# Groups of stick-breaking heads moved in among the last projections of a layer

## The chip, the cores and the metric

One NeuronCore of a Trainium2 chip runs the whole program. The metric is device time in microseconds (us), the median of several executions of the same program; lower is better. Five engines work from queues of their own, each strictly in its written order: TensorE (PE) multiplies, ScalarE (ACT) applies functions and copies, VectorE (DVE) does elementwise work, GpSimd (POOL) and SyncE (SP) mostly start transfers. They meet only at semaphores.

## The reference

256 tokens of width 1024 pass through two transformer layers and a third block, all in fp32. The second layer's mixer (`mixer_cd`) is the place of the change:

```python
def mixer_cd(h, w_in, w_out, rel_table):
    proj = h @ w_in                      # columns: qc, kc, vc, qd, kd, vd
    ...
    o_c = moba_attention(...)            # 8 heads; at 256 tokens: causal softmax with a bias
    o_d = stick_breaking_attention(...)  # 8 heads
    return jnp.concatenate([o_c, o_d], axis=-1) @ w_out

def stick_breaking_attention(q, k, v):
        z = jnp.einsum('bqhd,bkhd->bhqk', qb, k).astype(jnp.float32) * scale
        strict = kpos[None, :] < tq[:, None]
        log_1m = jnp.where(strict, jax.nn.log_sigmoid(-z), 0.0)
        after = lax.cumsum(log_1m, axis=3, reverse=True) - log_1m
        w = jnp.where(strict, jnp.exp(jax.nn.log_sigmoid(z) + after), 0.0)
        o = jnp.einsum('bhqk,bkhd->bqhd', w.astype(dt), v)
```

## The kernel before

**Weights.** SP loads chunks of 1 MB (`raw`, five buffers, L2032). Each chunk has two halves; ACT rounds a half to `HI` (`high`, L940 is the helper of every activation), DVE takes the rest, `LO = raw - HI` (`low`, L1352), and PE multiplies with both. Six half-chunks fit in `HI`/`LO` at once. `Walk` is the planner that all engines run alike: `use(key, half)` prepares the half-chunk four places ahead of the one named, if its slot is free, and along the way DVE multiplies chunks of the modulation matrices (`gemv`, L1342). `walk.spare(n)` takes up to n modulation halves, if these are the next in the plan. Where this layer's attention calls it the next chunk is a weight (`cdo` 2), so there it does nothing.

**The layer, in order.** `linear_fm` makes projections `cd` 0 to 5 (queries and keys, into `FMT`), `values_only` makes `cd` 6 and 7 (values of the stick-breaking heads), `keys_values` makes `cd` 8 (keys and values of the softmax heads). ACT copies each out of PSUM when it is complete. Then comes the attention, six rounds on each engine.

- The softmax heads are six units, taken in pairs: `scores` (PE), `biased` (DVE: bias and row maximum), `exps` (ACT), `scaled` (DVE), `transposes` (PE), `moved` (ACT, out of PSUM), `values` (PE).
- The stick-breaking heads are four groups g of two heads: `stick_scores` (PE makes z; DVE adds the mask, L1740; ACT takes abs, exp and ln, three passes of 768 columns), `stick_sums` (DVE forms the logarithms, L1746; PE sums them over the keys; DVE adds, L1749; ACT takes exp), `stick_values` (PE). `stage` deals two of these steps to each round: groups 0 and 1 go through all three steps, then groups 2 and 3.
- PSUM has four working banks (`take`/`give`), handed out in turn. PE waits in `take` until the reader of a bank's last content is done.
- Two sets of buffers (`stick_flat`) hold z, a and the logarithms l of a group, so group g shares with g - 2. Groups 0 and 1 use the queries and keys of `cd` 2 and 4, groups 2 and 3 those of `cd` 3 and 5.

**After it.** When the last `values` is done, ACT copies the four accumulator banks to `HH` (`out_parts` 0 to 3), DVE makes `HLo` (L1434), and `out_half("cdo", (0, ..., 5), 0)` multiplies with the output matrix. It needs parts 0 and 1 before its first matmul. ACT then makes the SiLU of a condition row and goes on with the weights.

## Time and profile before

| | |
|---|---|
| median of 3 executions | 1266.91 us (1266.78 to 1272.68) |
| the profiled execution's own time | 1268.52 us |
| its span, first to last instruction | 1266.7 us |
| mean granted TensorE clock | 0.965 |
| PE busy | 1159.9 us, 92% |
| PE weight loads busy | 1049.2 us, 83% |
| DVE busy | 933.0 us, 74% |
| ACT busy | 589.4 us, 47% |
| POOL busy | 74.4 us, 6% |

Times in the trace are us from the span's start. The projections of this layer run from 406.4 to 462 us, the attention from 462 to 503.9, the output matrix from there to 528.
### The profile page before, as it was taken

To read this page: it belongs to the slowest core of one execution; us is meant where nothing else is said; L and a number is where in the kernel's file an instruction comes from. 1 tells how busy PE (TensorE), PEld (TensorE's weight loads), DVE (VectorE), ACT (ScalarE), POOL (GpSimd) and SP (SyncE) were. 2 spreads that over 40 slices of the span, in tenths; PEclk is the share of its full clock that TensorE was granted. 3 is DMA by queue.
4 is the path that set the end of the run, shared out by engine and by line. 5 is a ranking of instruction groups with operands and counts; after the bars stand their busy time and mean duration, and the time that the engine had idled before them with its cause. 6 is when DMAs were issued, how large, how long until landed. Compare 5 with 4: busy or idle time off the path is not lost.

```text
span 1266.7 us, 19978 instructions
## 1 busy us (share of the span) xinstructions
PE 1159.9 (92%) x8358; PEld 1049.2 (83%) x8358; DVE 933.0 (74%) x1630; ACT 589.4 (47%) x968; POOL 74.4 (6%) x106
## 2 busy tenths in 40 slices
PE   2798798999998977899999989999989988999996
PEld 1687468999897975699999979999979967999996
DVE  5967868888786955598888688887765957765445
ACT  1534655434355455554445464454452365444443
POOL 0000000000000000079000000000000000000000
PEclk8799899999999989999999999999999998999998
DMA  9982335788882960357889637779732452665730
GB/s 375 364 358 74 152 128 196 299 319 286 310 331 100 374 225 1 136 203 277 315 202 368 245 139 296 293 273 292 279 140 101 105 177 85 254 233 200 194 133 34
DMA packets 40810, 280.83 MB, mean 222 GB/s; under 512 B 4736, under 2 KB 5264, under 8 KB 7952
## 3 DMA queue, kind: packets, MB, share of 16 engines
q1 hardware_dynamic: 37296, 269.27, 58.5%
q0 software_dynamic: 2416, 7.92, 2.2%
q10 hardware_dynamic: 1008, 2.37, 0.5%
q8 instruction: 65, 1.06, 0.3%
q14 instruction: 25, 0.20, 0.1%
HBM read 277.91 MB, written 1.10 MB: 220 GB/s over the span
## 4 chain that ended last, share of the span: by engine, by line
PE 69%; DVE 19%; ACT 6%; DMA 5%; issue 1%; SPq 0%; DVEq 0%; ACTq 0%
PE PS L408 68%; DVE LO L1352 5%; DMA raw<-WS 4%; DVE raw L1342 4%; ACT HI L940 2%; DMA SC<-scratch 1%; DVE TMP L1417 1%; DVE SC L1556 1%; DVE TMP L1452 1%; DVE HLo L1412 1%; ACT HH L940 1%; ACT SQ L940 1%; ACT SC L940 1%; DVE SC L1541 1%; DVE RS L1556 1%
## 5 line engine op out<-in xcount | busy, mean ns | idle before, releaser
L408 PE MATMUL PS<-HH,HI 128*128 128x256 f32 x1748 | 502.0, 287 | 25.6 <-ACT HH L940 22.3
L408 PE MATMUL PS<-HLo,HI 128*128 128x256 f32 x1748 | 503.3, 288 | 0.9 <-DVE HLo L1412 0.3
L408 PE MATMUL PS<-HH,LO 128*128 128x256 f32 x1748 | 499.3, 286 | 0.0
L1352 DVE TENSOR_TENSOR LO<-raw,HI 128x1024 fp32r<-128x1024 f32 x340 | 403.8, 1226 | 116.1 <-ACT HI L940 115.9
L940 ACT ACTIVATE HI<-raw 128x1024 fp32r<-128x1024 f32 x340 | 339.8, 1048 | 93.8 <-PE PS L408 64.8
L408 PEld LDWEIGHTS PS<-HH,HI 128*128 128x128 f32 x1748 | 340.0, 195 | 34.9 <-DVE LO L1352 18.9
L408 PEld LDWEIGHTS PS<-HLo,HI 128*128 128x128 f32 x1748 | 339.3, 194 | 4.2 <-DVE HLo L1412 2.9
L408 PEld LDWEIGHTS PS<-HH,LO 128*128 128x128 f32 x1748 | 339.8, 194 | 3.4 <-issue 0.5
L1342 DVE CUSTOM_DVE_ANT_0 raw<-raw,CB,SM 128x1024 f32<-128x1024 f32 x168 | 210.5, 1285 | 24.5 <-DMA raw<-WS 24.5
L408 PE MATMUL PS<-HI,HDH 128*128 128x512 f32 x352 | 140.4, 399 | 0.0
L408 PE MATMUL PS<-HI,HDL 128*128 128x512 f32 x352 | 139.6, 397 | 0.0
L408 PE MATMUL PS<-LO,HDH 128*128 128x512 f32 x352 | 138.9, 395 | 0.0
L940 ACT ACTIVATE HDH<-FB 128x256 fp32r<-128x256 f32 x88 | 36.8, 418 | 210.1 <-DVE FB L1513 210.0
L940 ACT ACTIVATE FB<-PS 128x256 f32<-128x256 f32 (+1 forms) x94 | 37.8, 403 | 129.4 <-PE PS L408 129.3
L408 PEld LDWEIGHTS PS<-HI,HDL 128*128 128x128 f32 x352 | 66.4, 189 | 15.9
L940 ACT ACTIVATE SC<-PS 128x512 f32<-128x512 f32 (+3 forms) x65 | 36.2, 572 | 90.0 <-PE PS L408 68.5
L408 PEld LDWEIGHTS PS<-LO,HDH 128*128 128x128 f32 x352 | 66.5, 189 | 12.8
L408 PEld LDWEIGHTS PS<-HI,HDH 128*128 128x128 f32 x352 | 66.5, 189 | 12.6 <-DVE LO L1352 0.2
L1513 DVE TENSOR_TENSOR FB<-FB,PS 128x256 f32<-128x256 f32 x88 | 36.7, 416 | 52.1 <-ACT FB L940 52.0
L408 PE MATMUL PS<-HI,HH 128*128 128x512 f32 (+2 forms) x176 | 62.3, 354 | 10.2 <-DVE HLo L1434 5.8
L1516 DVE TENSOR_TENSOR HDL<-FB,HDH 128x256 fp32r<-128x256 f32 x88 | 37.7, 428 | 45.9 <-ACT HDH L940 45.9
L408 PE MATMUL PS<-LO,HH 128*128 128x512 f32 (+2 forms) x176 | 61.4, 349 | 0.0
(230 smaller groups left out, 1023.1 us busy)
## 6 DMA issues: line engine op xcount, KB each, us to landing
raw<-WS SPq DMA_DIRECT2D x255, 1024.0 KB, 5.5
SC<-scratch POOLq DMA_DIRECT2D x2, 1024.0 KB, 13.4
FB<-gates_out POOLq DMA_DIRECT2D x3, 512.0 KB, 5.1
SQ<-gates_out POOLq DMA_DIRECT2D x3, 512.0 KB, 9.4
X<-xT ACTq DMA_DIRECT2D x1, 1024.0 KB, 6.9
SC<-ssm POOLq DMA_DIRECT2D x2, 512.0 KB, 5.0
out<-TMP SPq DMA_DIRECT2D x2, 512.0 KB, 2.6
CB<-vecs SPq DMA_DIRECT2D x1, 512.0 KB, 6.5
```

The costliest lines, as they stand in the source:

```text
L408: return e.matmul(o, l, r, start=start, stop=stop, skip_group_check=True)
L940: return e.activation(o, a, f, **k)
L1342: e.tensor_tensor_reduce(x, x, CB[:, :], 1.0, S("mb")[:, c:c + 1], O.mult, O.add, MV[:, c:c + 1]) \
L1352: e.tensor_tensor(LO[:, s % HL, :], raw_half(j, h), HI[:, s % HL, :].bitcast(fp32), O.subtract).then_inc(*D.up(("lo", s)))
L1412: e.scalar_tensor_tensor(HLo[:, k, :], TMP[:, k, :], MV[:, sh + k:sh + k + 1], HH[:, k, :].bitcast(fp32), O.add, O.subtract).then_inc(*D.u ...
L1417: e.scalar_tensor_tensor(TMP[:, k, :], turned(k), AV[:, k:k + 1], RS[:, 3, :], O.mult, O.mult) \
L1452: e.tensor_tensor(gy[qt][:, c], PS[:, b, :], grow(tag)[:, c], O.mult).then_inc(*D.up(("gy", tag, b)))
L1513: e.tensor_tensor(HF[:, j % 2, :], SIL[:, j % 2, :], bank((key, 0))[:, 256:512], O.mult) \
L1516: e.tensor_tensor(HDL[:, j % 3, :], HF[:, j % 2, :], HDH[:, j % 3, :].bitcast(fp32), O.subtract) \
L1541: e.tensor_scalar(s3[:, n, :], s3[:, n, :], gg[:, n:n + 1], None, O.mult) \
L1556: e.tensor_tensor_reduce(s3[:, n, :], bank(("s", tag, i))[:, n * kw:(n + 1) * kw], BI[:, bh + h0 + n, bo:bo + kw], 1.0, sk[:, n:n + 1] if ...
```

## The change

On all three compute engines the six rounds and their `stage` list are replaced by a written order:

- `stick_scores(0)` stands right after the projections 0 to 5, `stick_scores(1)` between the halves of `cd` 6, `stick_sums(0)` between those of `cd` 7, `stick_scores(2)` after `cd` 7, `stick_sums(1)` and `stick_values(0)` between the halves of `cd` 8, `stick_sums(2)` after it. `keys_values` and `values_only` get an argument `between` for this on PE; ACT and DVE have their parts and their `use` calls written out in the matching order.
- The logarithms are written over a (`af`), so that three sets of buffers fit. Group g now shares with g - 3.
- The remaining units (`stick_scores(3)`, the values of 1, 2 and 3, the sums of 3, and all of the softmax heads) are in an order written by hand. `out_parts` 2 and 3, which depend only on the stick-breaking heads, are copied before the last softmax values.
- PE waits in `stick_scores` for the projections it reads, and in `stick_values(0)` and `(1)` for the copied values.

```diff
@@ -358,8 +358,8 @@
         AB = dense(0, 10, 0, 0, 0, gate=1, last=False) + dense(0, 11, 128, 0, 0, gate=2) \
             + dense(4, 12, 256, 8, 2, sink=True)
         CD = dense(0, 12, 0, 0, 0)
-        stick_flat = [(SC[:, 11904:12672], SC[:, 6656:7424], SC[:, 7424:8192]),
-                      (sqf[:, 0:768], sqf[:, 768:1536], flat(TMP[:, 0:3, :]))]
+        stick_flat = [(SC[:, 11904:12672], SC[:, 6656:7424]), (sqf[:, 0:768], sqf[:, 768:1536]),
+                      (SC[:, 7424:8192], flat(TMP[:, 0:3, :]))]
         stick_cube = [[x.rearrange("p (h n) -> p h n", h=2) for x in f] for f in stick_flat]
 
         Wv = [WVT[:, i, :] for i in range(22)]
@@ -477,19 +477,23 @@
                         i = mm(o(qt), l[0], x[1], False, stop and k == ks[-1])
                 i.then_inc(*P.up(("lin", key, half), used(key, half)))
 
-            def keys_values(key):
+            def keys_values(key, between=()):
                 ps = take((key, 0))
                 wt = [x.rearrange("p (k n) -> p k n", k=8) for x in weight(key, 0)]
                 for k in range(8):
                     i = mm3(ps[:, 0:256], [x[:, k, :] for x in wt], H2[k], k, k == 0, k == 7, key[0])
                 i.then_inc(*P.up(used(key, 0)))
+                for f, g in between:
+                    f(g)
                 wt = [x.rearrange("p (k n) -> p k n", k=8) for x in weight(key, 1)]
                 linear_tm(lambda qt: ps[:, 256 + qt * 128:384 + qt * 128], key, 1, range(8), wt, False, True)
                 banks.give((key, 0))
 
-            def values_only(key):
+            def values_only(key, between=()):
                 ps = take((key, 0))
                 for half in range(2):
+                    for f, g in between if half else ():
+                        f(g)
@@ -777,12 +781,10 @@
             modulate("cd", 56, (8, 4, 4))
             for i in range(6):
                 linear_fm(("cd", i), H2, "cd", 8, 2)
-            for i in range(2):
-                values_only(("cd", 6 + i))
-            keys_values(("cd", 8))
 
             def stick_scores(g):
                 ps = [take(("ss", g, i)) for i in range(2)]
+                w.wait_ge(*A.at(("proj", "cd", 4 + g // 2)))
                 for kt in range(2):
                     for i in range(2):
                         hs = slice(i * 64, i * 64 + 64)
@@ -794,7 +796,7 @@
                     banks.give(("ss", g, i))
 
             def stick_sums(g):
-                l3 = stick_cube[g % 2][2]
+                l3 = stick_cube[g % 3][1]
                 for i in range(2):
                     ps = take(("sc", g, i))
                     w.wait_ge(*D.at(("sf", g)))
@@ -804,8 +806,10 @@
                     banks.give(("sc", g, i))
 
             def stick_values(g):
-                a3 = stick_cube[g % 2][1]
+                a3 = stick_cube[g % 3][1]
                 w.wait_ge(*A.at(("sa", g)))
+                if g < 2:
+                    w.wait_ge(*A.at(("v", g)))
                 for kt in range(2):
                     for i in range(2):
                         c = 128 + (2 * g + i) * 64
@@ -813,21 +817,31 @@
                                a3[:, i, kt * 256:256 + kt * 128], kt == 1)
                 x.then_inc(*P.up(("sv", g)))
 
-            stage = [(f, g) for g0 in (0, 2) for f in (stick_scores, stick_sums, stick_values) for g in (g0, g0 + 1)]
-
-            def two_stages(i):
-                for f, g in stage[2 * i:2 * i + 2]:
-                    f(g)
-
-            for i in range(6):
-                if i < 3:
-                    scores("cd", CD, i)
-                if 1 < i < 5:
-                    transposes("cd", i - 2)
-                walk.spare(2)
-                two_stages(i)
-                if i > 2:
-                    values("cd", CD, i - 3)
+            stick_scores(0)
+            values_only(("cd", 6), [(stick_scores, 1)])
+            values_only(("cd", 7), [(stick_sums, 0)])
+            stick_scores(2)
+            keys_values(("cd", 8), [(stick_sums, 1), (stick_values, 0)])
+            stick_sums(2)
+            scores("cd", CD, 0)
+            walk.spare(2)
+            stick_scores(3)
+            stick_values(1)
+            scores("cd", CD, 1)
+            walk.spare(2)
+            stick_values(2)
+            transposes("cd", 0)
+            stick_sums(3)
+            scores("cd", CD, 2)
+            walk.spare(2)
+            transposes("cd", 1)
+            values("cd", CD, 0)
+            walk.spare(2)
+            stick_values(3)
+            values("cd", CD, 1)
+            transposes("cd", 2)
+            walk.spare(4)
+            values("cd", CD, 2)
             out_half("cdo", (0, 1, 2, 3, 4, 5), 0)
             out_half("cdo", (0, 1), 1)
             out_half("cdo", (6, 7), 0)
...
@@ -1122,8 +1132,12 @@
                                 .then_inc(*DUPED.up("in", by=16))
                 if n in (2, 4):
                     flip(n // 2 - 1)
+            use(("ab", 6), 0)
+            use(("ab", 6), 1)
             keys_values(("ab", 6), 0, "kv6")
-            values_only(("ab", 7), 128, ("fm", "ab"))
+            use(("ab", 7), 0)
+            use(("ab", 7), 1)
+            values(("ab", 7), 128, ("fm", "ab"))
             w.wait_ge(*P.at("gates"))
             fn(ge, bank("gates")[0:24, 0:256], F.Exp, scale=-1.0).then_inc(*A.up(("free", "gates")))
 
@@ -1202,12 +1216,9 @@
                 use(("cd", i), 0)
                 use(("cd", i), 1)
                 evacuate(("cd", i), flat(FMT[:, 2 * i:2 * i + 2, :]), ("proj", "cd", i), 0.125 if i < 2 else 1.0)
-            for i in range(2):
-                values_only(("cd", 6 + i), 128 + 256 * i, ("v", i))
-            keys_values(("cd", 8), 0, ("fm", "cd"))
 
             def stick_scores(g):
-                zf, af, lf = stick_flat[g % 2]
+                zf, af = stick_flat[g % 3]
                 w.wait_ge(*D.at(("sz0", g, 1)))
                 fn(af, zf, F.Abs).then_inc(*A.up())
                 w.wait_ge(*A.now())
@@ -1215,32 +1226,51 @@
                 w.wait_ge(*A.now())
                 fn(af, af, F.Ln, bias=1.0).then_inc(*A.up(("sl", g)))
 
-            def stick_sums(g):
-                zf, af, lf = stick_flat[g % 2]
+            def stick_weights(g):
+                zf, af = stick_flat[g % 3]
                 w.wait_ge(*D.at(("sz", g, 1)))
                 fn(af, zf, F.Exp).then_inc(*A.up(("sa", g)))
 
-            def stick_values(g):
-                pass
-
-            stage = [(f, g) for g0 in (0, 2) for f in (stick_scores, stick_sums, stick_values) for g in (g0, g0 + 1)]
-
-            def two_stages(i):
-                for f, g in stage[2 * i:2 * i + 2]:
-                    f(g)
-
-            for n in range(6):
-                for i in (2 * n - 4, 2 * n - 3):
-                    if 1 < n < 5:
-                        moved("cd", i)
-                for i in (2 * n, 2 * n + 1):
-                    if n < 3:
-                        exps("cd", i, *CD[i])
-                high(walk.spare(2))
-                two_stages(n)
+            use(("cd", 6), 0)
+            use(("cd", 6), 1)
+            stick_scores(0)
+            values(("cd", 6), 128, ("v", 0))
+            stick_scores(1)
+            use(("cd", 7), 0)
+            use(("cd", 7), 1)
+            values(("cd", 7), 384, ("v", 1))
+            stick_weights(0)
+            use(("cd", 8), 0)
+            use(("cd", 8), 1)
+            stick_scores(2)
+            stick_weights(1)
+            keys_values(("cd", 8), 0, ("fm", "cd"))
+            stick_weights(2)
+            exps("cd", 0, *CD[0])
+            exps("cd", 1, *CD[1])
+            high(walk.spare(2))
+            stick_scores(3)
+            exps("cd", 2, *CD[2])
+            exps("cd", 3, *CD[3])
+            high(walk.spare(2))
+            moved("cd", 0)
+            moved("cd", 1)
+            stick_weights(3)
+            high(walk.spare(2))
+            moved("cd", 2)
+            moved("cd", 3)
+            exps("cd", 4, *CD[4])
+            exps("cd", 5, *CD[5])
+            high(walk.spare(2))
+            w.wait_ge(*P.at(("sv", 3)))
+            out_parts("cdo", 2)
+            out_parts("cdo", 3)
+            high(walk.spare(4))
+            moved("cd", 4)
+            moved("cd", 5)
             w.wait_ge(*P.at(("v", "cd", 5)))
-            for i in range(4):
-                out_parts("cdo", i)
+            out_parts("cdo", 0)
+            out_parts("cdo", 1)
             w.wait_ge(*C2IN.at("cond"))
             fn(CB[:, :], CB[:, :], F.Silu).then_inc(*A.up("cact"))
             e.preload_act_table_set(LNEXP)
@@ -1727,49 +1757,74 @@
             ffn("f0", rates(), 4, "cd", (40, 1.0, S("nw")[:, 24:32]))
             add_normed("cd", "f0", 56, S("nw")[:, 32:40], False)
             modulate("cd", 48)
-            for i in range(9):
+            for i in range(6):
                 use(("cd", i), 0)
                 use(("cd", i), 1)
 
             def stick_scores(g):
-                zm = stick_cube[g % 2][0]
+                zm = stick_cube[g % 3][0]
                 for i in range(2):
                     w.wait_ge(*P.at(("ss", g, i)))
-                    if g > 1:
-                        w.wait_ge(*P.at(("sv", g - 2)))
+                    if g > 2:
+                        w.wait_ge(*P.at(("sv", g - 3)))
                     e.scalar_tensor_tensor(zm[:, i, :], bank(("ss", g, i))[:, 0:384], 0.125, C("smask"), O.mult,
                                            O.add).then_inc(*D.up(("free", ("ss", g, i)), ("sz0", g, i)))
 
+            def stick_logs(g):
+                zf, af = stick_flat[g % 3]
+                w.wait_ge(*A.at(("sl", g)))
+                e.scalar_tensor_tensor(af, zf, 0.0, af, O.max, O.add).then_inc(*D.up(("sf", g)))
+
             def stick_sums(g):
-                (zf, af, lf), zm = stick_flat[g % 2], stick_cube[g % 2][0]
-                w.wait_ge(*A.at(("sl", g)))
-                e.scalar_tensor_tensor(lf, zf, 0.0, af, O.max, O.add).then_inc(*D.up(("sf", g)))
+                zm = stick_cube[g % 3][0]
                 for i in range(2):
                     w.wait_ge(*P.at(("sc", g, i)))
                     e.tensor_tensor(zm[:, i, :], zm[:, i, :], bank(("sc", g, i))[:, 0:384], O.add) \
                         .then_inc(*D.up(("free", ("sc", g, i)), ("sz", g, i)))
 
-            def stick_values(g):
-                pass
-
-            stage = [(f, g) for g0 in (0, 2) for f in (stick_scores, stick_sums, stick_values) for g in (g0, g0 + 1)]
-
-            def two_stages(i):
-                for f, g in stage[2 * i:2 * i + 2]:
-                    f(g)
-
+            def unit(f, i):
+                f("cd", i, *CD[i])
+
+            use(("cd", 6), 0)
+            stick_scores(0)
+            use(("cd", 6), 1)
+            stick_scores(1)
+            stick_logs(0)
+            use(("cd", 7), 0)
+            stick_sums(0)
+            stick_logs(1)
+            use(("cd", 7), 1)
+            stick_scores(2)
+            use(("cd", 8), 0)
+            stick_sums(1)
+            stick_logs(2)
+            use(("cd", 8), 1)
             gate("f1", 64, 1.0, S("nw")[:, 40:48])
-            for n in range(6):
-                for i in (2 * n, 2 * n + 1):
-                    if n < 3:
-                        biased("cd", i, *CD[i])
-                for i in (2 * n - 2, 2 * n - 1):
-                    if 0 < n < 4:
-                        scaled("cd", i, *CD[i])
-                low(walk.spare(2))
-                two_stages(n)
-            for i in range(4):
-                out_parts("cdo", i)
+            stick_sums(2)
+            unit(biased, 0)
+            unit(biased, 1)
+            low(walk.spare(2))
+            stick_scores(3)
+            unit(biased, 2)
+            unit(biased, 3)
+            unit(scaled, 0)
+            unit(scaled, 1)
+            low(walk.spare(2))
+            stick_logs(3)
+            unit(scaled, 2)
+            unit(scaled, 3)
+            low(walk.spare(2))
+            stick_sums(3)
+            unit(biased, 4)
+            unit(biased, 5)
+            low(walk.spare(2))
+            unit(scaled, 4)
+            unit(scaled, 5)
+            low(walk.spare(4))
+            out_parts("cdo", 2)
+            out_parts("cdo", 3)
+            out_parts("cdo", 0)
+            out_parts("cdo", 1)
             linear_out("cdo", range(8))
             add_normed("f1", "cdo", 80, S("nw")[:, 48:56], True)
             modulate("f1", 72)
```

## Rows read from the trace of the kernel before

**Rows 1.** Busy time by stretch: stretch, its us, each engine's busy us (instructions), PEclk, DMA share, GB/s
```profile
406.40:462.00 55.60, 55.58 (x448) 54.99 (x448) 44.00 (x60) 23.96 (x31) 1.46 (x2) 0.97 0.84 331
462.00:503.90 41.90, 26.16 (x192) 20.17 (x193) 24.58 (x83) 26.22 (x60) 0.54 (x1) 0.88 0.07 14
```

**Rows 2.** Waits of TensorE from 462 to 504 us: total us, times, longest
```profile
PE PS L408 <- DVE SC L1746: 7.0, 2, 5.1
```

**Rows 3.** Timeline of TensorE: start us, us, engine, line, operation, out<-in, count [idle before <-releaser]
```profile
466.59 0.92 PE L408 MATMUL PS<-SC 64*128 64x256 f32 x8 [1.95 <-DVE SC L1556]
...
479.89 0.70 PE L408 MATMUL PS<-TMP,CN 128*128 128x256 f32 x2 [1.51 <-DVE TMP L1746]
...
481.84 1.13 PE L408 MATMUL PS<-SC 64*128 64x256 f32 x8
...
482.90 1.09 PE L608 MATMUL PS<-CN,SC 128*128 128x128 f32 x8
...
483.93 0.87 PE L408 MATMUL PS<-SC 128*64 128x256 f32 x8
...
484.63 0.82 PE L408 MATMUL PS<-SQ,SC 128*64 128x256 f32 x8
...
503.92 0.47 PE L408 MATMUL PS<-HI,HH 128*128 128x512 f32 x1 [2.14 <-ACT HH L940]
```

**Rows 4.** Timeline of ScalarE, columns as before
```profile
442.31 0.60 ACT L940 ACTIVATE SC<-PS 128x512 f32<-128x512 f32 x1 [3.27 <-PE PS L408]
...
448.56 2.00 ACT L940 ACTIVATE HI<-raw 128x1024 fp32r<-128x1024 f32 x2
...
466.95 0.39 ACT L940 ACTIVATE SC<-SC 128x128 f32<-128x128 f32 x1
...
468.49 2.58 ACT L940 ACTIVATE SC<-SC 128x768 f32<-128x768 f32 x3
...
473.46 0.49 ACT L940 ACTIVATE SC<-SC 128x256 f32<-128x256 f32 x1
...
479.00 0.84 ACT L940 ACTIVATE SC<-SC 128x768 f32<-128x768 f32 x1 [3.48 <-DVE SC L1749]
...
483.60 1.08 ACT L940 ACTIVATE SC<-PS 128x512 f32<-128x512 f32 x2 [0.22 <-PE PS L608]
...
501.86 2.06 ACT L940 ACTIVATE HH<-PS 128x512 fp32r<-128x512 f32 x4 [1.86 <-PE PS L408]
```

**Rows 5.** Timeline of VectorE
```profile
463.99 0.35 DVE L1556 CUSTOM_DVE_ANT_0 SC<-PS,SC,eps 128x128 f32<-128x128 f32 x1 [6.02 <-PE PS L408]
...
466.55 1.01 DVE L1740 SCALAR_TENSOR_TENSOR SC<-PS,CN 128x384 f32<-128x384 f32 x2
...
469.71 0.48 DVE L1556 CUSTOM_DVE_ANT_0 SC<-PS,SC,eps 128x256 f32<-128x256 f32 x1 [1.17 <-PE PS L408]
...
471.72 0.17 DVE L1535 RECIPROCAL SC<-SC 128x4 f32<-128x4 f32 x1
...
473.71 0.95 DVE L1746 SCALAR_TENSOR_TENSOR SC<-SC 128x768 f32<-128x768 f32 x1
...
476.89 0.55 DVE L1749 TENSOR_TENSOR SC<-SC,PS 128x384 f32<-128x384 f32 x1 [2.23 <-PE PS L408]
...
485.21 0.62 DVE L1541 TENSOR_SCALAR SC<-SC 128x256 f32<-128x256 f32 x2
...
502.49 2.48 DVE L1434 TENSOR_TENSOR HLo<-PS,HH 128x512 fp32r<-128x512 f32 x4 [3.37 <-ACT HH L940]
```

**Rows 6.** Busy time by stretch again, columns as in rows 1: three stretches of the attention and after
```profile
474.80:478.40 3.60, 3.57 (x12) 3.02 (x12) 0.55 (x1) 0.72 (x4) 0.00 (x0) 0.55 0.00 0
...
490.00:500.00 10.00, 6.47 (x48) 5.29 (x48) 4.14 (x7) 6.81 (x10) 0.00 (x0) 1.00 0.00 0
...
505.15:508.80 3.65, 3.65 (x11) 2.82 (x9) 0.11 (x1) 3.61 (x5) 0.00 (x0) 0.53 0.02 4
```

**Rows 7.** Timeline of GpSimd: the transfer that fetches the gate row for f1
```profile
469.73 0.54 POOL L1939 DMA_DIRECT2D FB<-gates_out  x1 [10.56 <-DMA gates_out<-GV]
```

More of the change, by code:

```diff
@@ L1004, in keys_values @@
             def keys_values(key, dst, ev):
-                use(key, 0)
-                use(key, 1)
                 ps = bank((key, 0))
@@ L1011, in keys_values, with values @@
                     .then_inc(*A.up(("free", (key, 0)), ev))
-            def values_only(key, dst, ev):
-                use(key, 0)
-                use(key, 1)
+            def values(key, dst, ev):
                 w.wait_ge(*P.at(("lin", key, 1)))
```

## The prediction

> **What bounds the kernel now.** I first read the busy times by stretch and then who waits in the weak stretch. In the projections (406.4 to 462 us) PE is busy 55.58 of 55.60 us, DVE 44.0 and ACT 24.0. In the attention (462 to 503.9) PE is busy 26.2 of 41.9 us, DVE 24.6, ACT 26.2 [rows 1]. So the first stretch is bound by PE and has room on the other two; the second is bound by no engine but by a chain that passes from one to another. The waits of PE say where: 7.0 us of its 15.7 idle us are waits for the logarithms of L1746, one of them 5.1 us [rows 2]. The transfers bound neither: in the attention the DMA engines are busy 7% [rows 1], because the five buffers are full.
>
> **What moves, and its price on PE.** A change of order removes no matmul. Moved in among the projections are three times `stick_scores`, twice `stick_sums`, once `stick_values`. `stick_scores` is 8 records that take 0.92 us with the tail of the last, 0.8 to the next start. `stick_sums` runs from 479.89 to 481.84, 1.95 us at the full clock. `stick_values` runs from 483.93 to 484.63, 0.7 us [rows 3]. Sum: 3 x 0.8 + 2 x 1.95 + 0.7 = 7.0 us. As PE has no gap there, its projections end 7.0 us later, at 469.0. In return the three groups' waits for DVE and ACT should lie beside 20 us of projection work, and the attention starts with one group's weights made and two groups' nearly so.
>
> **Do the moved steps wait inside the projections?** `cd` 5 ends at about 442.3 (its copy starts at 442.31), and a projection takes some 5.8 us, a half of `cd` 6 or 7 so 2.88 (the copy in [rows 4]; 48 of the 448 records that take 55.6 us in [rows 1] for cd 5, the same for the others but cd 8). PE: scores(0) to 443.1, scores(1) at 445.9, sums(0) at 452.5, scores(2) at 457.3, sums(1) at 461.0, values(0) at 463.0, end of `cd` 8 at 469.0, sums(2) there. What each needs, with a pair of mask additions at 0.95 us (1.01 with the last one's tail) [rows 5], the three ACT passes at 2.5 and a last exp at 0.84 [rows 4], the logarithms at 0.95 and an addition at 0.55 [rows 5]:
> - ACT rounds the halves of `cd` 8 until 444.8, as it does `cdo` 0 at 448.56 now [rows 4]; DVE takes the rests at 443.9 and 446.0 with the mask of group 0 between them (446.0). ACT has a, exp and ln of group 0 at 448.6, DVE the logarithms at 449.6: 2.9 us before sums(0).
> - ACT is then held until 449.6 by the copy of `cd` 6, does group 1 until 452.8 and only then the halves of `cdo` 0 (454.8). DVE waits for them, so its additions for group 0 end at 456.1 and the logarithms of group 1 at 457.1: 3.9 us before sums(1). The bank that scores(2) takes is free at 455.6, 1.7 us early; this is the tightest one.
> - The weights of group 0 are ready at 458.9 (values(0): 463.0), the logarithms of group 2 at 464.6 (sums(2): 469.0).
>
> All have 1.7 us or more to spare, so I cost the insertions at nothing beyond PE's 7.0 us. If the cover were gone, a miss would stand one to one on PE. Between the two shapes of matmul the trace shows no exchange as such; bounds for each insertion are 0 (the steps of 479 to 485 follow without a gap, rows 3) and 0.1 us, so 0 to 0.6 us in all. I take 0.
>
> **The moved halves and queues.** On ACT and DVE the splitting of `cdo` 0 and 1 now stands behind stick work and ends at 458.3 and 465.8, some 6 to 8 us later than now. The output matrix is not touched before 492. SP's next loads wait for these rests and start as much later; the attention leaves the DMA engines idle [rows 1], so they land well ahead. The gate row for f1 is written and fetched by POOL: the fetch starts at 469.73 now, after 10.56 us of waiting for its write [rows 7]; its factor is formed 8 us later, so the fetch starts at some 478, and the row is wanted only behind the output matrix. The last modulation product ends at 452.0 by this order; its reader, the SiLU, stands behind out_parts. All hidden. The logarithms written over a are the same instruction on 768 columns: 0 (below nothing there is no reason either, since read and written sizes stay).
>
> **The attention that is left,** from the same prices. A 4-head unit costs DVE 1.28 us in `biased` (463.99 to 466.55 for two) and 1.0 in `scaled` (471.72 to 473.71 for two); a 2-head unit 1.0 (469.71 to 471.72 for two) and 0.7 (0.62 for its two multiplications, and a reciprocal) [rows 5]. `exps` costs ACT 1.55 (466.95 to 468.49 for a 4-head unit's last four passes) or 0.98 (two of 0.49), `moved` 0.5 [rows 4]. On PE a pair's scores take 1.06, its transposes 1.03 [rows 3], its values 0.8 like the 8 records of rows 3.
> - sums(2) until 471.0, scores of pair 0 until 472.0, scores(3), values(1) until 473.5. DVE adds for group 2 until 471.7, then biased 0 and 1 until 474.7. The scores of pair 1 need the bank of unit 1: 474.6 to 475.7, then values(2).
> - DVE is now the bound: mask of group 3 (475.6), biased 2 and 3 (477.8), scaled 0 and 1 (479.8), logarithms of group 3 (480.8; ACT's ln is there at 479.2). PE turns units 0 and 1 as they come and does sums(3) from 480.85 to 482.8.
> - Scores of pair 2 until 483.9, transposes of pair 1, values 0, values(3), values 1 until 487.2. DVE: biased 4 and 5 until 486.0. ACT: exps 4 and 5 until 487.6. DVE: scaled 4 and 5 at 487.4 and 488.4. PE: transposes until 488.9. ACT: out_parts 2 and 3 in between, then moved 5 until 489.75. PE: values of pair 2 from 489.8, and ACT's out_parts 0 at 490.9.
> - From there to the first output matmul it is 503.92 - 501.86 = 2.06 us, as now [rows 3, 4]: parts 0 and 1 were always the ones that PE waited for, so having 2 and 3 done early saves nothing here. The start is at 492.95.
>
> That is 503.92 - 492.95 = 11.0 us earlier at the full clock. Behind it the output matrix, f1 and the rest have the same work and waits, shifted as a whole.
>
> **The clock.** From 474.8 to 478.4 the granted clock is 0.55 and sums(0) takes 3.6 us instead of 1.95, after a PE that was idle 5.1 us [rows 2, 6]. From 490 to 500 PE is busy 65% and the clock stays at 1.00 [rows 6]. In my order PE is busy about 3.2 of the 6.9 us from 473.5 to 480.4, its longest gap 2.5 us. That lies between the two rows; nearer to the first by its share. A fall then meets sums(3), on the path, for 3.55 - 1.95 = 1.6 us (bounds 0 and, with the next scores also at half, 2.7). I take 1.6. After the last values the clock falls already now, 0.53 from 505.15 to 508.80, which costs about 1.65 us [rows 6]; PE is idle as long there as before, so I leave that in.
>
> **Sum:** -11.0 + 1.6 = -9.4 us. The profiled execution goes from 1268.52 to 1259.1; it lies 1.6 above the median of the runs shown, so the median goes from 1266.91 to 1257.5 us.
>
> One rule speaks against it. Rows 1 say that PE has 15.7 us to give in this stretch. The Trainium skill's page "Perfetto Trace Analysis" (section "Identifying the Most-Contended Engine") says to find the engine with the highest occupancy and to work on that one first. For the whole program that is PE, which this change gives nothing less to do; by the rule read so, the sum would be near 0, by the rows of the stretch it is what stands above. I follow the rows, since the occupancy of the whole hides the one stage.
>
> **Rivals.**
> - *The clock holds.* PE gets no long idle stretch and stays at 2.4 GHz, also at the output matrix: -11.0 - 1.65 = -12.6, 1254.3 us. For it: 490 to 500 in rows 6. Against: the many short gaps that DVE leaves. Chance 0.17. The page "TensorE: Matmul & The Clock Gate" of the Trainium skill (section "HAM oscillation — how this bites in real kernels") tells of gaps after which bursts start slow each time, which would speak for a fall.
> - *The clock falls and stays low* from 474 to the output matrix, since DVE's bound of 472 to 488 keeps PE half idle. Then sums(3), the scores and transposes of pair 2 and its values double on the path: 1.95 + 1.06 + 0.5 + 0.8 + 0.5 = 4.8 us, so -11.0 + 4.8 = -6.2: 1260.7 us. For it: the low clock of rows 6, which held until 478.4 with PE at work for 3.6 us. Chance 0.15.
> - *The change doesn't do what it says:* a step in my order waits for something that I passed over, so that only the 7.0 us of rows 2 are gained, and new waits like the two I find for PE (1.1 us for the banks of pair 1, 0.45 before sums(3)) take some 2 us back: about -5, 1262 us. Chance 0.08.
> - *Slower:* the inserted steps hold up the projections. DVE stands in its queue behind `HI` of `cdo` 0, ACT behind the copy of `cd` 6; if sums(0) came 3 us late and each of the four steps behind it likewise, PE would lose 5 x 3 = 15 us while projecting, and this eats 9.4. It decides from 1.9 us per step; my smallest margin is 1.7 us on the good side. +5: 1272 us. Chance 0.04.
>
> **How the numbers follow.** Forecast 0.56, rivals 0.17, 0.15, 0.08 and 0.04. The forecast's own range is 1255.5 to 1259.5 (bounds 0 to 0.6 for the insertions, 0 to 2.7 for the clock). The 8-in-10 range takes in the two clock rivals and goes about 1.3 us beyond each, for the bank wait of 1.1 us that either may lack or have twice: 1253 to 1262. A measurement of this kernel tells about 0.5% (6.3 us) from no change, so "faster" means under 1260.6: forecast, the first rival, and not quite half of the second, 0.8. Same 0.17, slower 0.03.
>
> **What would show it.** Right: projections with PE busy throughout, ending near 469; DVE busy from 471 to 488; first output matmul near 493; out_parts 2 and 3 before it. Wrong: idle time of PE between 442 and 469; the clock at 0.5 after 483; a wait of PE for `HI`/`LO` at the output matrix or in f1 that is longer than now.

## The result, and the profile after

| | before | after |
|---|---|---|
| median | 1266.91 us (5 runs, 1266.24 to 1272.68) | 1259.00 us (5 runs, 1257.63 to 1261.30) |
| ratio | | 0.9921, 95% interval 0.9904 to 0.9939 |
| the profiled execution | 1268.52 us | 1258.39 us |
| span | 1266.7 us | 1256.6 us |
| from the copy of projection 5 to the first output matmul | 61.6 us | 52.6 us |

The change takes 7.9 us off the median, 0.8%; 9.4 was forecast. The last line of the table is what I call the stretch from here on: from ScalarE's copy of `cd` 5, the last step ahead of the new order, to the first matmul with the output matrix. All experiments are read by it, since profiles of one order of steps give it within 0.9 us (52.5 in e11, 53.3 in e5), while whole executions of one program differ by several us.

TensorE after the change, busy time by stretch, columns as in [rows 1]. The first two lines answer to those of [rows 1], the last two to [rows 6]:

```profile
406.40:469.90 63.50, 63.44 (x508) 61.20 (x508) 51.99 (x74) 33.31 (x42) 1.46 (x2) 0.98 0.75 287
469.90:495.30 25.40, 18.20 (x137) 13.15 (x137) 18.01 (x71) 18.02 (x50) 0.54 (x1) 0.92 0.10 30
481.60:485.00 3.40, 3.37 (x14) 2.89 (x14) 1.91 (x7) 1.29 (x4) 0.00 (x0) 0.57 0.21 78
495.30:499.30 4.00, 4.00 (x12) 3.22 (x13) 0.20 (x1) 3.96 (x5) 0.00 (x0) 0.64 0.02 4
```

The projections with the moved steps now last until 469.9, still with PE busy throughout. Behind them are 25.4 us, where there were 41.9, and PE is busy 72% of them instead of 62%. The waits of PE from 442 to 496 (total us, times, longest), to be held against the 7.0 us of [rows 2] and one more line of the kernel before, for group 1, whose logarithms lay in `TMP`:

```profile
PE PS L408 <- DVE TMP L1746: 1.5, 1, 1.5
```

After the change:

```profile
PE PS L612 <- DVE SC L1565: 2.4, 1, 2.4
PE PS L408 <- DVE HLo L1464: 2.1, 1, 2.1
PE PS L408 <- DVE SC L1586: 1.2, 1, 1.2
PE PS L408 <- ACT SC L954: 0.8, 1, 0.8
PE PS L612 <- DVE SC L1571: 0.5, 2, 0.3
```

None of them is a wait for the logarithms, which had 8.5 us before; 2.4 us is for `scaled` 0, 1.2 for the banks of pair 1, and 2.1 the output parts, as before. The timeline of TensorE:

```profile
442.57 0.92 PE L408 MATMUL PS<-SC 64*128 64x256 f32 x8
...
443.43 0.39 PE L408 MATMUL PS<-HI,HH 128*128 128x256 f32 x1
...
446.49 0.70 PE L408 MATMUL PS<-SC 64*128 64x256 f32 x4
...
453.19 0.59 PE L408 MATMUL PS<-SC,CN 128*128 128x256 f32 x2
...
457.90 0.92 PE L408 MATMUL PS<-SC 64*128 64x256 f32 x8
...
461.73 0.59 PE L408 MATMUL PS<-SQ,CN 128*128 128x256 f32 x2
...
469.79 0.65 PE L408 MATMUL PS<-TMP,CN 128*128 128x256 f32 x2
...
475.48 1.13 PE L408 MATMUL PS<-SC 64*128 64x256 f32 x8 [1.18 <-DVE SC L1586]
...
479.85 0.63 PE L612 MATMUL PS<-CN,SC 128*128 128x128 f32 x4 [2.44 <-DVE SC L1565]
...
481.63 1.22 PE L408 MATMUL PS<-SC,CN 128*128 128x256 f32 x2
...
484.98 1.14 PE L408 MATMUL PS<-SC 64*128 64x256 f32 x8
...
492.11 1.08 PE L408 MATMUL PS<-SC 128*64 128x256 f32 x8 [0.78 <-ACT SC L954]
...
495.30 0.77 PE L408 MATMUL PS<-HI,HH 128*128 128x512 f32 x1 [2.11 <-DVE HLo L1464]
```

stick_scores(0) and (1) at 442.57 and 446.49, sums(0) at 453.19, stick_scores(2) at 457.90, sums(1) at 461.73: no bracket with an idle time on any. ScalarE and VectorE beside it:

```profile
442.68 0.60 ACT L954 ACTIVATE SC<-PS 128x512 f32<-128x512 f32 x1 [3.27 <-PE PS L408]
...
469.99 0.66 ACT L954 ACTIVATE SC<-PS 128x256 f32<-128x256 f32 x2 [4.87 <-PE PS L408]
...
477.38 2.98 ACT L954 ACTIVATE SC<-SC 128x768 f32<-128x768 f32 x4
...
493.24 1.08 ACT L954 ACTIVATE HH<-PS 128x512 fp32r<-128x512 f32 x2 [1.27 <-PE PS L408]
```

```profile
449.09 0.96 DVE L1776 SCALAR_TENSOR_TENSOR SC<-SC 128x768 f32<-128x768 f32 x1 [0.61 <-ACT SC L954]
...
455.72 1.01 DVE L1782 TENSOR_TENSOR SC<-SC,PS 128x384 f32<-128x384 f32 x2
...
472.88 0.35 DVE L1586 CUSTOM_DVE_ANT_0 SC<-PS,SC,eps 128x128 f32<-128x128 f32 x1 [0.53 <-PE PS L408]
...
480.62 0.96 DVE L1776 SCALAR_TENSOR_TENSOR SC<-SC 128x768 f32<-128x768 f32 x1
```

### The profile page after: what moved, and what is told of

Same layout as the page of the kernel before. It is cut to its first block, busy times and chain, and to the rows that moved or that the text cites. A ratio compares the mean times of both kernels' runs of the same rounds, so it can differ in the third digit from the quotient of the medians.

```text
span 1256.6 us, 19977 instructions
## 1 busy us (share of the span) xinstructions
PE 1159.3 (92%) x8358; PEld 1049.2 (83%) x8358; DVE 933.0 (74%) x1630; ACT 589.3 (47%) x968; POOL 74.7 (6%) x106
## 4 chain that ended last, share of the span: by engine, by line
PE 72%; DVE 17%; DMA 5%; ACT 5%; issue 1%; SPq 0%; DVEq 0%; ACTq 0%
PE PS L408 71%; DVE LO L1382 5%; DMA raw<-WS 4%; DVE raw L1372 3%; ACT HI L954 2%; DMA SC<-scratch 1%; DVE TMP L1482 1%; DVE SC L1586 1%; DVE TMP L1447 1%; DVE HLo L1442 1%; ACT SQ L954 1%; DVE SC L1571 1%; ACT HH L954 1%; ACT SC L954 0%; DVE RS L1586 0%
## 5 line engine op out<-in xcount | busy, mean ns | idle before, releaser
L1546 DVE TENSOR_TENSOR HDL<-FB,HDH 128x256 fp32r<-128x256 f32 x88 | 37.8, 429 | 45.9 <-ACT HDH L954 45.9
L408 PE MATMUL PS<-HI,HLo 128*128 128x512 f32 (+2 forms) x176 | 61.6, 350 | 0.0
```

Of the source, the lines that this page charges most:

```text
L408: return e.matmul(o, l, r, start=start, stop=stop, skip_group_check=True)
L1546: e.tensor_tensor(HDL[:, j % 3, :], HF[:, j % 2, :], HDH[:, j % 3, :].bitcast(fp32), O.subtract) \
```

## The experiments

**Is it the placement or the order? The steps moved back behind the projections** (e2):

```diff
-            stick_scores(0)
-            values_only(("cd", 6), [(stick_scores, 1)])
-            values_only(("cd", 7), [(stick_sums, 0)])
-            stick_scores(2)
-            keys_values(("cd", 8), [(stick_sums, 1), (stick_values, 0)])
+            values_only(("cd", 6))
+            values_only(("cd", 7))
+            keys_values(("cd", 8))
+            stick_scores(0)
+            stick_scores(1)
+            stick_sums(0)
+            stick_scores(2)
+            stick_sums(1)
+            stick_values(0)
             stick_sums(2)
```

and likewise on the other two engines.

> The changed kernel with its three buffer sets and its hand order, but every stick step that it put among projections 6, 7 and 8 stands behind projection 8, in the same order. Theory (the gain is the three groups' round trips hidden beside projections): the round trips come back; sums(2) starts at about 475 on the scale of the trace before instead of 470, the stretch is about 58 us (57 to 60), 5 to 6 more than after the change. Rival (the hand order and the third buffer set are the gain): 54 or less.

Measured: stretch 60.4 us (442.24 to 502.64), 1266.36 us against 1266.19 of the kernel before beside it, ratio 0.9996 (0.9982 to 1.001). The waits of its PE:

```profile
PE PS L408 <- DVE SC L1777: 4.1, 2, 3.9
PE PS L612 <- DVE SC L1566: 2.4, 1, 2.4
PE PS L408 <- DVE HLo L1465: 2.1, 1, 2.1
PE PS L408 <- DVE TMP L1777: 1.8, 1, 1.8
...
PE PS L408 <- DVE SQ L1777: 0.5, 1, 0.5
```

The waits for the logarithms (L1777) are back. In the stretch the hand order, the third buffer set and the early parts together are worth 1.2 us, the placement 7.8: 6.1 are the waits ahead of sums(0), (1) and (2) (3.9, 0.5 and 1.8), and 1.3 the low clock in sums(0), which took 3.25 us instead of 1.95. Whole executions say the same of the placement, with ratios of 0.9996 and 0.9921 whose intervals lie apart, but can't tell the 1.2 us from nothing, and in the stretch it is hardly more than the 0.9 by which profiles differ. The placement needs the third set, since group 2 starts before the values of group 0; what that set is worth by itself was not run. My number was 2.4 too low: sums(2) started at 477.1, not 475, since sums(0) ran at the low clock as it does before the change. From sums(2) to the end it took 25.6 us, as in the changed kernel (469.79 to 495.30).

**The rest dealt to rounds again** (e3):

```diff
-            scores("cd", CD, 0)
-            walk.spare(2)
-            stick_scores(3)
...
-            values("cd", CD, 2)
+            rest = [[(stick_scores, 3), (stick_values, 1)], [(stick_values, 2)], [(stick_sums, 3)], [(stick_values, 3)], [], []]
+            for i in range(6):
+                if i < 3:
+                    scores("cd", CD, i)
+                if 1 < i < 5:
+                    transposes("cd", i - 2)
+                for f, g in rest[i]:
+                    f(g)
+                if i > 2:
+                    values("cd", CD, i - 3)
```

> The steps among the projections stay where the change put them; what is left is dealt to six rounds as before the change (scores of pairs 0, 1, 2 in rounds 0, 1, 2, transposes two rounds later, values one more, the output parts last). Theory (the placement is the gain, the order behind it is worth little): 52 to 54 us, since VectorE has the same work to do in it. Rival (the hand order matters): 56 or more.

Measured: 54.7 us, 1261.44 us, ratio 0.9951 (0.9930 to 0.9971). That lies between the two theories: on top of the placement the hand order is worth 2.0 us in one profile of each. The median is 2.4 us above the changed kernel's, but the intervals of the ratios overlap. One line of its PE timeline says how:

```profile
485.70 1.19 PE L408 MATMUL PS<-SC,CN 128*128 128x256 f32 x2 [3.75 <-DVE SC L1755]
```

The logarithms of group 3 stand behind `biased` 4 and 5 and `scaled` 2 and 3 in VectorE's queue, so PE waits 3.75 us for them, and its sums then run at the low clock. In the hand order the logarithms come first (480.62 above) and the wait is gone.

**The early output parts** (e1):

```diff
-            w.wait_ge(*P.at(("sv", 3)))
-            out_parts("cdo", 2)
-            out_parts("cdo", 3)
...
-            out_parts("cdo", 0)
-            out_parts("cdo", 1)
+            for i in range(4):
+                out_parts("cdo", i)
```

> The changed kernel, but all four output parts are copied after the last softmax values, in the order 0, 1, 2, 3, as before. Measure: the stretch from the copy of projection 5 to the first output matmul, 61.6 us before the change (442.31 to 503.92) and 52.6 after it (442.68 to 495.30). Theory (PE waits only for parts 0 and 1): 52.6, within 0.3. Rival (the early parts 2 and 3 are a part of the gain, as two copies less stand in ScalarE's queue): 53.6 or more, two copies of 0.5 us later.

Measured: 52.8 us, 1258.46 us, ratio 0.9934 (0.9911 to 0.9957). They are worth nothing that can be told, as the step in the prediction had it.

**How much cover there is.** The absolute value of groups 0 to 2 taken three times (e9) and six times (e10):

```diff
+                for _ in range(2 if g < 3 else 0):
+                    fn(af, zf, F.Abs).then_inc(*A.up())
+                    w.wait_ge(*A.now())
                 fn(af, zf, F.Abs).then_inc(*A.up())
```

This is e9; e10 has a 5 in place of the 2.

> The changed kernel with the absolute value of groups 0, 1 and 2 taken three times instead of once, which adds 2 x 0.84 us to ScalarE's part of each round trip and changes no number. It tells how much cover the projections give. Theory (the insertions have 1.7 us and more to spare, the tightest being the bank of stick_scores(2)): PE waits 0 to 0.5 us in the projections, stretch 52.6 to 53.2. Rival (the insertions are on the path already and PE's lack of gaps there is luck of the order): 54.3 or more.

Measured: stretch 52.3 us, 1256.99 us (2 runs), ratio 0.9908 (0.9872 to 0.9943). 1.7 us more in each of three round trips cost PE one wait of 0.4 us, at stick_scores(2), the place with the smallest margin. That the stretch is no longer than the changed kernel's is the clock's doing: sums(3) took 2.49 us here (480.00 to 482.49) instead of 3.35. The output matrix ran at clock 1.00, though nothing had been done for it:

```profile
492.80:497.00 4.20, 4.18 (x19) 3.49 (x20) 0.38 (x1) 4.16 (x5) 0.00 (x0) 1.00 0.01 4
...
510.87 1.28 DVE L1494 SCALAR_TENSOR_TENSOR X<-TMP,NR,X 128x1024 f32<-128x1024 f32 x1
```

The second line is the first normed row, 18.1 us after the first output matmul at 492.82; in the changed kernel it is 19.4.

> The changed kernel with the absolute value of groups 0, 1 and 2 taken six times, 5 x 0.84 = 4.2 us more in each of the three round trips; the numbers stay the same. The margins of my prediction are 2.9, 1.7 and 3.9 us. Theory (beyond them a miss stands one to one on PE): PE waits 1 us before stick_sums(0), some 3 before stick_scores(2), 4 to 6 in all in the projections; stretch 56.5 to 59. Rival (the queues of ScalarE and VectorE soak it up): under 54.

Measured: 60.6 us, 1263.96 us (one execution; 1265.03 for the kernel before beside it). PE's waits, and a window of its projections:

```profile
PE PS L408 <- DVE SC L1785: 4.2, 1, 4.2
...
PE PS L408 <- DVE SC L1779: 1.2, 1, 1.2
...
461.00:466.00 5.00, 4.95 (x24) 4.63 (x24) 4.44 (x6) 4.36 (x5) 0.00 (x0) 0.50 0.27 80
```

The waits are 1.2 us before sums(0) and 4.2 before stick_scores(2), where I had 1 and some 3. What I had left out is the third line: behind the long wait PE works at half the clock for 5 us, which costs 2.5 more. So this miss cost more than one to one.

**The clock.** Eighteen matmuls on zeros in the changed kernel's longest wait (e4), and 6 and 18 of them in its last two waits (e5); `busy(n)` issues 2n:

```diff
+            busy(9)
             transposes("cd", 0)
...
+            busy(3)
             values("cd", CD, 2)
+            busy(9)
```

The first line is e4, the other two are e5.

> The changed kernel with 18 matmuls on zeros (256 columns, results never read) ahead of the transposes of pair 0, where PE waits 2.44 us for VectorE. Theory (the clock falls at 480 because PE is half idle from 475 on, and the fall costs the sums of group 3 their 1.4 us): granted clock 1.00 through stick_sums(3), which takes 1.95 us instead of 3.35, and a stretch (copy of projection 5 to first output matmul) of 51.2 us instead of 52.6. Rival (the fall is owed to the later or smaller gaps, or these small products don't count as work): the clock falls all the same and the stretch is 52.6 or up to 1 us longer.

Measured: stretch 51.2 us, 1254.43 us (2 runs), ratio 0.9887 (0.9858 to 0.9917).

```profile
475.77 2.14 PE L408 MATMUL PS<-zeros 128*128 128x256 bf16 x18
...
478.28 0.63 PE L612 MATMUL PS<-CN,SC 128*128 128x128 f32 x4 [0.37 <-DVE SC L1566]
...
480.05:482.00 1.95, 1.95 (x12) 1.73 (x13) 1.79 (x7) 1.26 (x4) 0.00 (x0) 1.00 0.10 40
...
492.30:497.00 4.70, 4.67 (x21) 3.91 (x22) 0.87 (x1) 4.66 (x5) 0.00 (x0) 1.00 0.02 3
```

The fillers take 2.14 us of the wait, the transposes still wait for VectorE, sums(3) is through in 1.95 us at clock 1.00. The five other profiles of these steps without this filler (e1, e5, e9, e10, e11) had 2.49 to 3.67 us there, the changed kernel's first 3.35, so for the middle the filler is the likely cause, on one profile with it. And the output matrix keeps 1.00 too, without a filler of its own: from the first output matmul to the first normed row it takes 18.1 us instead of 19.4.

> The changed kernel with 6 such matmuls ahead of the last softmax values and 18 behind them, in PE's last two waits (0.8 and 2.1 us). Theory: the clock stays at 1.00 in the output matrix, whose records from 495.9 to 499 take 0.43 us each now and would take 0.23; the stretch stays 52.6, and the time from the first output matmul to the first part of the normed rows shrinks by about 1.6 us. Rival: the fall comes from what lay before these waits, and stays.

Measured: 53.3 us, then 18.1 us to the first normed row; 1256.24 us (2 runs), ratio 0.9902 (0.9870 to 0.9934).

```profile
479.00:486.90 7.90, 6.87 (x28) 5.54 (x28) 5.19 (x18) 4.72 (x13) 0.00 (x0) 0.57 0.16 66
496.20:500.00 3.80, 3.80 (x17) 3.15 (x18) 0.01 (x1) 3.76 (x5) 0.00 (x0) 1.00 0.02 4
```

The output matrix stays at 1.00. But so it did in e4 and e9, which have no filler there; the other nine profiles without one had it low. Two profiles with end fillers (e5 and e8) and both at 1.00 speak for them and don't show it. The low clock in the middle lasted twice as long in this profile (0.57 over 7.9 us), which is the stretch's 0.7 more, against the 52.6 that I expected, and not the fillers' doing, since they stand behind it.

The same in the kernel before (e12):

```diff
                 walk.spare(2)
+                if i == 1:
+                    busy(20)
                 two_stages(i)
```

> The kernel before the change with 40 matmuls on zeros (4.3 us) in PE's wait of 5.1 us ahead of stick_sums(0). Theory (half of that gap's price is the wait itself, the rest the low clock behind it, and the wait is ended by VectorE whatever PE does): the wait is still over at the same time, sums(0) takes 1.95 us instead of 3.6, and the stretch is 60.0 instead of 61.6. So of the change's 9.0 us some 1.6 were there to be had by the clock alone. Rival: sums(0) starts late behind the fillers or the clock stays low; 61.6 or more.

Measured: 62.4 us (442.46 to 504.88), 1269.17 us (one execution; 1265.03 for the kernel before beside it). Busy time of two windows; the first is sums(0), the second the same 10 us as in [rows 6]:

```profile
474.90:478.30 3.40, 1.95 (x14) 1.66 (x12) 1.97 (x3) 1.59 (x5) 0.00 (x0) 1.00 0.00 0
...
490.00:500.00 10.00, 6.97 (x30) 5.89 (x32) 3.96 (x6) 4.52 (x7) 0.00 (x0) 0.66 0.01 2
```

sums(0) takes 1.95 us, and the steps behind it come 1.7 us earlier. But now the clock falls from 492 on, in the stretch that kept 1.00 before at much the same share of busy time, and sums(2) and (3) take the gain back and 0.8 more. The time lies in the rival's range, but not by its mechanism: the low clock was not taken away but came at another place.

The theory also had the order of things wrong. In the kernel before the clock had fallen ahead of the long wait, in stick_scores(1):

```profile
467.71 2.02 PE L408 MATMUL PS<-SC 64*128 64x256 f32 x8 [0.20 <-DVE SC L1740]
...
467.60:470.00 2.40, 2.02 (x8) 1.29 (x8) 1.23 (x3) 2.37 (x8) 0.27 (x1) 0.54 0.00 0
```

These 8 records take 0.92 us at the full clock [rows 3]. The 40 fillers of e12, which start at 469.27, met the same low clock (0.50 from 469.2 to 471.0) and took 5.82 us, not 4.3; from 472 on they ran at 1.00, while the kernel before had 0.50 through the whole wait. What went before the fall was a PE busy 1.8 of the 4 us from 462 to 466, with no wait over 2.0 us.

**One more profile of the changed kernel** (e11).

> The changed kernel once more, nothing altered, to see how much a second profile of one program differs. The order is fixed, so the work between the waits takes the same; only where the clock falls may shift: stretch 52.6, within 0.6, and 19.4 or 18.0 us from the first output matmul to the first normed row.

Measured: stretch 52.5, then 21.0 us to the first normed row, which is more than either value I expected, 1262.74 us. The stretch repeats within 0.2. But the copy of projection 5 comes at 444.58 us here and at 442.68 in the first profile, before any changed instruction has run. Two windows of this profile say why:

```profile
407.50:414.50 7.00, 6.93 (x31) 6.44 (x30) 6.81 (x15) 3.93 (x6) 0.00 (x0) 0.51 0.05 6
...
497.00:503.20 6.20, 6.15 (x15) 4.84 (x16) 2.36 (x2) 4.72 (x5) 0.00 (x0) 0.50 0.01 3
```

In the first profile the same places had the low clock for about half as long (0.53 from 406.0 to 409.6, and 0.54 from 495.3 to 498.4). The two are 3.4 of the 4.3 us by which these executions of one program differ.

**The keys early** (e7): the softmax keys are copied when the first half of `cd` 8 is done, and the first softmax scores join the projections. On PE:

```diff
-            keys_values(("cd", 8), [(stick_sums, 1), (stick_values, 0)])
-            stick_sums(2)
-            scores("cd", CD, 0)
+            ...  # first half of cd 8, bank given back
+            stick_sums(1)
+            stick_values(0)
+            stick_scores(3)
+            scores("cd", CD, 0)
+            stick_sums(2)
+            ...  # second half, queries 0 to 127, in a bank of its own
+            scores("cd", CD, 1)
+            ...  # second half, queries 128 to 255
+            stick_sums(3)
+            scores("cd", CD, 2)
+            transposes("cd", 0)
+            stick_values(1)
+            stick_values(2)
+            transposes("cd", 1)
```

> One step further in the same direction. The keys of the softmax heads are copied after the first half of projection 8, whose second half gets a PSUM bank of its own; the scores of pairs 0 and 1, stick_scores(3) and stick_sums(2) stand before or between the parts of the second half. Theory (behind the projections the stretch is bound by the passage from one engine to the next, and PE has idle time to lose): 46 us (45 to 48.5), 6 to 7 less than after the change, and PE idle less than 4 us in it outside of the last 2. Rival (VectorE's own work from the masks on is the bound, so moving PE's work earlier brings nothing): 51 or more.

Measured: 45.9 us, 1252.52 us, ratio 0.9891 (0.9868 to 0.9914).

```profile
440.80:484.60 43.80, 42.97 (x361) 37.77 (x360) 34.25 (x95) 32.59 (x67) 2.07 (x3) 1.00 0.46 160
...
PE PS L408 <- DVE HLo L1479: 2.1, 1, 2.1
...
PE PS L408 <- ACT SC L969: 0.8, 1, 0.8
```

From the copy of `cd` 5 to the end of the last transposes PE is busy 43.0 of 43.8 us at clock 1.00; what is left of its waits is 0.8 us for the last `moved` and 2.1 for the output parts. The stretch is bound by PE now, but for these 2.9 us.

With the two end fillers on top (e8):

> The version with the keys copied early and the same fillers at its end. Theory: stretch 45.9 us as in that version, clock 1.00 in the output matrix, 1.6 us less than that version's 1252.5: about 1251. Rival: no difference, since the clock falls anyway.

Measured: 45.9 us, and 18.1 us to the first normed row instead of e7's 19.7; 1249.53 us, ratio 0.9844 (0.9820 to 0.9869), against the changed kernel's 0.9921. This is the fastest version. How much of its 3.0 us over e7 are the fillers' is open, as for e5.

## Why the prediction was right, step by step

- **What bounds it.** That a chain bound the attention and PE the projections was right; e7 shows it from the other side, since with the chain hidden the stretch falls until PE binds.
- **The price on PE, 7.0 us.** It was 7.6: the softmax keys are copied 27.3 us after `cd` 5 (442.68 to 469.99), before the change 19.7. I took 0 from a bound of 0 to 0.6 for the insertions, and the upper end was right in sum, but not piece by piece: a `stick_scores` cost 1.05 and not 0.8, well over the 0.1 that I allowed an insertion, while sums(0) cost 1.76 and not 1.95, and the last two steps 2.7 for 2.65. That these met at 0.6 is in part luck. The seam is seen at 442.57: the group starts 0.20 us after the last projection record (0.12 is their pace) and 0.86 us pass to the next record at 443.43, and the second record follows after 0.22.
- **No waits among the projections.** Right, and with the margins: sums(0) started 3.1 us after its logarithms (449.09 + 0.96; I had 2.9), and stick_scores(2), at 457.90, 1.7 us after its bank (first half of the pair at 455.72 done by 456.2; I had 1.7). e9 used up the smaller one and found a wait of 0.4 us there.
- **The attention that is left.** From the last projection to the first output matmul I had 23.95 us and 1.6 for the clock, 25.5; it took 25.4. VectorE was the bound between 472.88 and 483, as worked out. I had it busy until 488; from 483 on it waited three times for PE (0.7, 0.8 and 0.5 us), which worked without a gap until 490.4. Most of that is the low clock in sums(3): in e4, where it held, VectorE waited for PE only twice there (0.2 and 0.5 us).
- **The clock.** Right in place and size: 0.57 from 481.6 to 485, sums(3) 3.35 us instead of 1.95, so 1.4 where I took 1.6. In e4 it held and the 1.4 came back. The reason I gave was weaker than its number: I read the fall at 474.8 as following the wait of 5.1 us, but the clock was at 0.54 before that wait began. And in the same steps the loss was between 0.5 (e9) and 1.7 us (e5) from profile to profile, so that 1.4 came so near to 1.6 is in part luck. That the fall behind the last values stays was right in this profile; in e4 and e9 it didn't happen.
- **The sum.** 9.0 us in the stretch against 9.4 forecast: 0.6 too little for the insertions, 0.2 too much for the clock. The median moved by 7.9 and this profiled execution by 10.1; the rest of the program had the same work, and e11 shows that the length of a low clock elsewhere makes such differences. The waits for logarithms that I set against the change were 8.5 us and not the 7.0 of the one row I quoted; the sum doesn't use them, only the rival of 1262 us does.
- **The rule on the most contended engine** would have had no gain. The Trainium skill's page "Perfetto Trace Analysis" (section "Optimization Strategy") also says that a kernel may have regimes with different contended engines and that interleaving them can help. By that second rule the trace agrees: e2, which undoes the interleaving alone, gives back 7.8 of the 9.0 us.
- **The rivals.** "The clock holds" didn't happen, but in e4 it did, and its price was right: 1254.4 us measured (2 runs), 1254.3 forecast. "The clock stays low" didn't happen. "Slower" was priced wrongly: e10 has two of its waits, 5.4 us, and pays 8.0, as the clock falls in the projections. At that rate, 1.5 us for each us of wait, it would by my estimate decide near 1.3 us per step and not 1.9; a version so late in all five steps was not run.

## What to carry to other kernels

When one stage keeps an engine full and the next is a chain between engines, move the chain's first links into the full stage, at seams where their inputs have been ready for longer than one queue's delay. Work out the margin of each inserted step against everything that stands ahead of it in the other engines' queues, the banks too; a missed margin on PE costs the wait and can cost a low clock behind it (8.0 us for waits of 5.4 in e10). Behind the move, the order within the loose stage is a second, smaller gain (2.0 us here): an instruction on which PE waits goes ahead of work that nobody waits for yet.

## What was not expected of the hardware

- Matmuls on zeros whose results nobody reads cost nothing where PE waited anyway, and the three profiles of the new order with them (e4, e5, e8) had the clock at 1.00 right behind them: 1.4 us gained in the middle, and 1.4 to 1.6 at the output matrix. For the middle six profiles without them are the comparison, all with a low clock; at the output matrix it also held in two without, so there it isn't shown. In e12 it held for some 17 us behind them and then fell.
- Whether a loosely filled stretch keeps its clock isn't told by its busy share alone. From 490 to 500 the kernel before kept 1.00 at 65% [rows 6]; 1.7 us earlier, in e12, nearly the same steps had 0.66 at 70%, busier only because they ran slower. Nor does one long wait tell: before the change the clock fell ahead of the wait of 5.1 us. Profiles of the same step order (after, e5 up to its fillers, e11) had different lengths of low clock. What decides it stays open.
